# Block-sparse sample attention on one core: gathers, scores and denominators placed anew

## The chip, the cores and the metric

The kernel runs on one core of a Trainium2 chip. The metric is the device time of one execution in microseconds (us), less being better. The program is one inference step of a two-layer decoder trunk, for a prompt of 512 tokens and a sample group of 8 sequences with 8 new tokens each. All data are f32.

Names of the engines: PE (TensorE, matmuls and transposes through the identity), DVE (VectorE), ACT (ScalarE), POOL (GpSimd, which also issues the gathers), SP (SyncE, which issues the plain DMAs). Each engine runs its own instructions strictly in order; semaphores tie them together.

## The reference, cut to what matters

The change touches the sample half of branch B: compressed keys, selected blocks of 64 rows, and a window of 512 rows, each a softmax attention of its own.

```python
def ab_sample(...):
    kcf = concatenate([gather_pages(cc_k, page_table), kc])      # 4096 past rows of each sequence
    o_cmp, p_cmp = cmp_attend(qb, compress(kcf, pe_k, w1_k, w2_k), compress(vcf, ...), qpos)
    idx = select_blocks(p_cmp, qpos, ...)                        # the 16 best blocks for each query
    o_slc = slc_sample(qb, cs_k, cs_v, ks, vs, page_table, idx, qpos, sl_b)
    o_win = win_sample(qb, kwb, vwb, qpos, past_len, sl_b)

def compress(k, pe, w1, w2):      # blocks of 32 rows, flattened
    return silu((k + pe) @ w1) @ w2

def masked_softmax(s, valid):
    m = max(s); p = where(valid, exp(s - m), 0); den = sum(p)
    return p / den, m, den
```

## The kernel before

The stages follow one another, with a barrier between them: projection, prompt attention, sample attention A, then `compress_sample` (L1163), `attend_sample_b` (L1313), then the merge of the branches, the recurrence of layer 1 and the output projection. The change lies in the two named ones.

**compress_sample.** There are 16 units: 8 sequences, keys and values. For each, POOL gathers 4096 rows (2 MB, one indirect DMA with the page indices `idx`, L1202) into one of two buffers and regroups them by KV head (L1188); PE transposes them (L1230) and multiplies them with the compression weights (L1239). POOL issues a gather two units ahead; at the last two units it issues none.

**attend_sample_b.** The keys of the selected blocks are not gathered one by one: for every sequence b all 4096 rows of K and V are fetched (`xk`, `xv`, 2 MB each, two buffers each, L1417), and rows outside the 16 chosen blocks get a bias of -1e30. The work is a software pipeline of passes. In pass b, PE

- turns the keys of sequence b: eight groups of 512 rows (`keys`, L1468) and the window (`window_keys`, L1475), PSUM banks `bT`, copied to SBUF by DVE (groups 0, 1, 2, 3, 5, 7) or ACT (4, 6 and the window);
- computes their scores (`scores`, 128x512 in three banks `bS`, L1491, "w" for the window L1488, "n" for the new tokens L1485);
- turns the softmax weights of sequence b-1 (`turn`, L1498) out of `sc`, and multiplies them with its values (`weigh`, L1522; `weigh_rest` for window, new tokens and compressed blocks, L1532 to L1542);
- prepares the choice of blocks of sequence b+1 (`blocks` L1455, `groups` L1459).

DVE adds the bias to every score group and takes its minimum (`add_bias`, L1726, into `sc`), forms `nmax` (L1774, L1775), and for sequence b+1 the probabilities (`block_weights`, L1700, L1701) and the choice (`select`, L1706 to L1717). ACT takes the exponentials (`exp`, L1623, two groups each) and copies banks. POOL builds the bias `bd` of sequence b+1 (eight instructions, L1429) and issues the gathers. `outputs` (L1740 to L1745) divides by the denominators `den`, `den4`, of which there is one set.

The order is written out by hand in each engine's program, and the list `fills` gives the order in which `bT` banks are used. In pass b the scores of groups 0 to 3 stand on PE between the last weights' turns, "w", "n" and 4 to 7 stand at its end. `sc` holds one sequence: DVE may write the scores of b only when the weights of b-1 have been turned out of it, for which it waits once, for the last turn ("Pn").

At the stage's start SP loads the queries, old keys (`setup_in`) and five tables (`const_ready`), then the windows; POOL issues four gathers (K and V of sequences 0 and 1) at once. PE waits for `setup_in`, turns the queries, and then needs `const_ready`.

## Time and profile before

| what | us |
|---|---|
| median of 3 runs (2525.16 to 2527.83) | 2526.34 |
| the profiled execution, its own time | 2522.46 |
| its span | 2520.7 |
| PE busy in the span | 2228.4 |
| compress_sample (PE's first to last matmul) | 1057.5 to 1238.0 |
| attend_sample_b (PE's first to last matmul) | 1264.8 to 1499.1 |

PE is busy for 88% of the span, DVE 34%, ACT 28%, POOL 13%. Below, a "pass" begins where `blocks` (L1455) of the next sequence begins on PE. Columns of a timeline row: start in us, length in us, engine, line, operation, output<-inputs, shape, count; in brackets the idle time of that engine just before it and who ended it. A line of n instructions merged is followed by xn.

### The profile page before, as it was taken

To read this page: it belongs to the slowest core of one execution; us is meant where nothing else is said; L and a number is where in the kernel's file an instruction comes from. 1 tells how busy PE (TensorE), PEld (TensorE's weight loads), DVE (VectorE), ACT (ScalarE), POOL (GpSimd) and SP (SyncE) were. 2 spreads that over 40 slices of the span, in tenths; PEclk is the share of its full clock that TensorE was granted. 3 is DMA by queue.
4 is the path that set the end of the run, shared out by engine and by line. 5 is a ranking of instruction groups with operands and counts; after the bars stand their busy time and mean duration, and the time that the engine had idled before them with its cause. 6 is when DMAs were issued, how large, how long until landed. Compare 5 with 4: busy or idle time off the path is not lost. (4 is left out here: it accounts for less than half of the span.)

```text
span 2520.7 us, 34463 instructions
## 1 busy us (share of the span) xinstructions
PE 2228.4 (88%) x13652; PEld 1359.5 (54%) x13652; DVE 854.5 (34%) x2146; ACT 717.1 (28%) x1452; POOL 315.9 (13%) x393
## 2 busy tenths in 40 slices
PE   6999999478897788599679979969999999999798
PEld 3444454364444566488556654436666666566443
DVE  0000000025664344233254422324545444454322
ACT  0001000025664323122135430013444434343300
POOL 0000001103453000144143311000000000000000
PEclk9999999659999899799889989979999999999899
DMA  3232322302112999655334429048988897989710
GB/s 110 75 107 103 80 73 64 58 19 66 51 39 79 415 406 411 243 210 201 119 142 167 156 76 250 0 93 254 290 260 291 248 297 251 300 257 323 251 74 21
DMA packets 207823, 436.87 MB, mean 173 GB/s; under 512 B 59744, under 2 KB 162992, under 8 KB 191024
## 3 DMA queue, kind: packets, MB, share of 16 engines
q1 hardware_dynamic: 199856, 359.29, 43.8%
q0 software_dynamic: 7808, 75.39, 7.9%
q8 instruction: 109, 1.79, 0.3%
q14 instruction: 50, 0.41, 0.1%
HBM read 410.04 MB, written 163.13 MB: 227 GB/s over the span
## 5 line engine op out<-in xcount | busy, mean ns | idle before, releaser
L1901 PE MATMUL rec_bR<-x1T,rec_w 128*128 128x512 f32 x768 | 355.6, 618 | 0.0
L1901 PEld LDWEIGHTS rec_bR<-x1T,rec_w 128*128 128x128 f32 x768 | 147.4, 197 | 172.1 <-issue 171.1
L230 PE MATMUL pab_acc<-xT,pab_w 128*128 128x512 f32 x512 | 224.1, 598 | 10.0 <-DMA pab_w<-in_w_in_ab 10.0
L230 PEld LDWEIGHTS pab_acc<-xT,pab_w 128*128 128x128 f32 x512 | 97.4, 192 | 132.9 <-issue 122.7
L1136 DVE MEMSET kc_p<- 128x32 f32 x1 | 0.1, 85 | 471.2 <-PE cmpp_bP L1082 471.2
L234 PE MATMUL pab_acc<-pab_w,xT 128*128 128x512 f32 (+1 forms) x384 | 155.3, 565 | 0.0
L1239 PE MATMUL cmp_bH<-cmp_xT,cmp_w 128*128 128x256 f32 x512 | 131.5, 382 | 0.0
L548 ACT ACTIVATE ap_sc<-ap_sc,ap_nmax 128x128 f32<-128x128 f32 (+1 forms) x192 | 106.2, 554 | 84.3 <-DVE ap_nmax L578 83.1
L726 PE MATMUL mab_acc<-mab_w,mab_hT 128*128 128x512 f32 x256 | 114.8, 608 | 12.7 <-DMA mab_hT<-scratch_h 12.7
L2276 PE MATMUL out_acc<-out_w,oT 128*128 128x512 f32 x256 | 112.3, 601 | 13.5 <-DMA out_w<-in_w_out_c 13.5
L887 PE MATMUL sa_bT<-ident,sa_ring 128*128 128x128 f32 x640 | 88.8, 298 | 33.2 <-DMA sa_ring<-in_cache_a_k 24.2
L1910 PE MATMUL rec_bR<-rec_w,x1T 128*128 128x128 f32 x1024 | 117.0, 275 | 0.0
L1910 PEld LDWEIGHTS rec_bR<-rec_w,x1T 128*128 128x128 f32 x1024 | 115.7, 192 | 0.5 <-issue 0.5
L234 PEld LDWEIGHTS pab_acc<-pab_w,xT 128*128 128x128 f32 x384 | 72.5, 190 | 80.5 <-issue 80.5
L2105 POOL TENSOR_TENSOR rec_v_own<-rec_rows,rec_row_own 64x512 f32<-64x512 f32 x16 | 16.5, 1032 | 779.4 <-PE rec_bX L1960 631.7
L578 DVE CUSTOM_DVE_ANT_0 ap_sc<-ap_bS,ap_bias 128x128 f32<-128x128 f32 (+1 forms) x192 | 86.5, 488 | 68.4 <-PE ap_bS L493 32.9
L887 PEld LDWEIGHTS sa_bT<-ident,sa_ring 128*128 128x128 f32 x640 | 79.0, 154 | 44.3 <-DMA sa_ring<-in_cache_a_k 27.7
L516 PE MATMUL ap_bT<-ident,ap_sc 128*128 128x128 f32 x480 | 73.7, 285 | 30.2 <-ACT ap_pT L563 18.7
L1230 PE MATMUL cmp_bT<-ident,cmp_xg 128*128 128x128 f32 x512 | 78.8, 281 | 22.6 <-POOL cmp_xg L1188 20.6
L516 PEld LDWEIGHTS ap_bT<-ident,ap_sc 128*128 128x128 f32 x480 | 53.0, 143 | 75.9 <-POOL ap_sc L612 69.4
L1274 DVE COPY cmp_xT<-cmp_bT 128x512 f32<-128x512 f32 x80 | 55.3, 692 | 112.2 <-PE cmp_bT L1230 112.2
L1239 PEld LDWEIGHTS cmp_bH<-cmp_xT,cmp_w 128*128 128x128 f32 x512 | 88.7, 192 | 7.1
(368 smaller groups left out, 3448.2 us busy)
## 6 DMA issues: line engine op xcount, KB each, us to landing
out<-in_cache_a_k SPq DMA_DIRECT2D x8, 8160.0 KB, 29.7
out<-in_cache_a_v SPq DMA_DIRECT2D x8, 8160.0 KB, 29.6
sa_ring<-in_cache_a_k SPq DMA_DIRECT2D x40, 1024.0 KB, 12.6
sa_ring<-in_cache_a_v SPq DMA_DIRECT2D x40, 1024.0 KB, 20.4
rec_w<-in_w_in_c SPq DMA_DIRECT2D x64, 512.0 KB, 6.8
pab_w<-in_w_in_ab SPq DMA_DIRECT2D x8, 2048.0 KB, 8.1
pab_w<-in_w_in_ab SPq DMA_DIRECT2D x64, 128.0 KB, 3.3
ap_bias<-in_bias_p SPq DMA_DIRECT2D x16, 512.0 KB, 4.2
```

The costliest lines, as they stand in the source:

```text
L230: last = nc.tensor.matmul(acc[a % 8][:, :], w[u][:, k, j * P:(j + 1) * P], xT[:, k, 0:SEQ], start=(k == 0), stop=(k == KD - 1))
L234: last = nc.tensor.matmul(acc[a % 8][:, 0:width], xT[:, k, j * P:(j + 1) * P], w[u][:, k, 0:width], start=(k == 0), stop=(k == KD - 1))
L516: last = nc.tensor.transpose(bT[h][:, j * P:(j + 1) * P], sc[(i - LAG) % RING][h][:, j * P:(j + 1) * P], ident[:, :])
L548: nc.scalar.activation(at, at, ACT.Exp, bias=nmax[:, i % RING, h:h + 1], scale=-1.0, accum_out=den[:, i % RING, h:h + 1]).then_inc(exp_don ...
L578: nc.vector.tensor_tensor_reduce(out=sc[i % RING][h][:, 0:cols], in0=bS[i % 2][h][:, 0:cols], in1=bias[grp % 2][:, h, SEQ - cols:SEQ], sca ...
L726: last = nc.tensor.matmul(acc[m % 2][half][:, :], hT[:, k, m * P:(m + 1) * P], w[:, k, 512 * half:512 * half + 512], start=(k == 0), stop= ...
L887: last = nc.tensor.transpose(bank[:, (2 * jj + t) * P:(2 * jj + t + 1) * P], ring[at % RING][:, t, j * P:(j + 1) * P], ident[:, :])
L1230: last = nc.tensor.transpose(bT[f % 4][:, j * P:(j + 1) * P], xg[u][:, g, k * P:(k + 1) * P], ident[:, :])
L1239: last = nc.tensor.matmul(bH[i % 2][:, 0:KVB * P], w1[i % 2][:, k, :], xT[i % 2][:, k, :, :].rearrange("p g n -> p (g n)"), start=(k == 0) ...
L1901: last = nc.tensor.matmul(bank[:, :], w[h % 2][:, at, k, :], xT[:, k, 0:SEQ], start=(k == 0), stop=(k == KD - 1))
L1910: last = nc.tensor.matmul(bank[:, m * P:(m + 1) * P], xT[:, k, m * P:(m + 1) * P], w[h % 2][:, V_AT, k, :], start=(k == 0), stop=(k == KD ...
L2276: last = nc.tensor.matmul(acc[m % 2][half][:, :], oT[:, k, m * P:(m + 1) * P], w[:, k, 512 * half:512 * half + 512], start=(k == 0), stop= ...
```

## The change

1. **Gathers of sequence 0.** Where `compress_sample` issued no gather (its last two units), POOL now gathers K and V of sequence 0 of the selected branch into two tensors `first_k`, `first_v`, which live over both stages and serve as buffer 0 of `xk`, `xv`. In `attend_sample_b` POOL waits for `const_ready` and `setup_in` and then issues the two gathers of sequence 1.
2. **Order of the scores.** PE's loop over the eight groups is now: turn the weights of b-1, turn the keys of b, scores of the group before, weigh the group before. The scores run 0 to 7, then "w", "n"; `weigh(b-1, 7)` and `weigh_rest` stand at the pass's end.
3. **Finer waits.** `add_bias(b, j)` waits for the turn of group j of sequence b-1, not for the last turn. On DVE the adds stand between the copies of keys, `outputs(b-1)` stands behind `nmax` of b.
4. **Two sets of denominators** (`den4`, `den`): `exp` waits for the outputs of two sequences back.

```diff
@@ compress_sample, gpsimd
                     if i + 2 < NU:
                         pool.wait_ge(grouped[u], 2 * b + 2)
                         gather(i + 2)
+                    else:
+                        pool.indirect_dma_start(first[u][:, :, :].rearrange("p c k -> p (c k)"), None,
+                                                next_rows[u].rearrange("e n (s c) g d -> (e n s) (c g d)", c=CB),
+                                                bass.IndirectOffsetOnAxis(ap=idx[:, 0:1], axis=0)).then_inc(first_in[u], 16)
@@ attend_sample_b
-        xk, xv = ([s.sb(f"{n}{u}", [P, NKT, P]) for u in range(2)] for n in ("xk", "xv"))
+        xk, xv = ([x, s.sb(n, [P, NKT, P])] for x, n in zip(first, ("xk1", "xv1")))
-        den4, den, rden, cden = s.sb("den4", [P, 4]), s.sb("den", [P, 3]), s.sb("rden", [P, 3]), s.sb("cden", [P, 2])
+        den4, den, rden, cden = s.sb("den4", [P, 2, 4]), s.sb("den", [P, 2, 3]), s.sb("rden", [P, 3]), s.sb("cden", [P, 2])
-        SCORES = (0, 1, 2, 3, "w", "n", 4, 5, 6, 7)
+        SCORES = (0, 1, 2, 3, 4, 5, 6, 7, "w", "n")
@@ gpsimd
-                for b in range(2):
-                    gather(b, xk, pool_rows[0], xk_in)
-                    gather(b, xv, pool_rows[1], xv_in)
                 pool.wait_ge(const_ready, 16 * 5)
+                pool.wait_ge(setup_in, 16 * 4)
+                for x, rows, ready in ((xk, pool_rows[0], xk_in), (xv, pool_rows[1], xv_in)):
+                    gather(1, x, rows, ready)
@@ tensor, after keys(b, 0..2)
+                    for j in range(TC):
                         if before:
                             turn(b - 1, j)
+                        if mine and j < 5:
                             keys(b, 3 + j)
+                        if mine and j == 5:
+                            window_keys(b)
+                        if mine and j >= 1:
+                            scores(b, j - 1)
                         if before and j >= 1:
                             weigh(b - 1, j - 1)
+                        if after and j == 2:
+                            groups(b + 1)
                     if before:
                         turn_window(b - 1)
+                        turn_new(b - 1)
                     if mine:
+                        for j in (7, "w", "n"):
+                            scores(b, j)
                     if before:
                         weigh(b - 1, 7)
                         weigh_rest(b - 1)
@@ scalar
-                        if b >= 2:
-                            act.wait_ge(o_read, b - 1)
+                        if b >= 3:
+                            act.wait_ge(o_read, b - 2)
@@ vector, add_bias
+                    if b >= 1:
+                        dve.wait_ge(turned, number[{"w": ("Pw", b - 1, 0), "n": ("Pn", b - 1, 0)}.get(j, ("P", b - 1, j))] + 1)
@@ vector, a pass
                         copy_keys(b, 3)
+                        add_bias(b, 0)
                         copy_keys(b, 5)
+                        add_bias(b, 1)
                     if after:
                         select(b + 1)
                     if mine:
+                        add_bias(b, 2)
                         copy_keys(b, 7)
-                        if b >= 1:
-                            dve.wait_ge(turned, number["Pn", b - 1, 0] + 1)
-                        for j in SCORES[:4]:
-                            add_bias(b, j)
-                    if before:
-                        outputs(b - 1)
-                    if mine:
-                        for j in SCORES[4:]:
+                        for j in SCORES[3:]:
                             add_bias(b, j)
                         dve.wait_ge(s_read, len(SCORES) * (b + 1))
                         line(nc.vector.tensor_reduce(nmax[:, 1:2], low_w[:, :], AX_X, ALU.min))
                         nc.vector.tensor_reduce(nmax[:, 0:1], low[:, :], AX_X, ALU.min).then_inc(max_ready, 1)
+                    if before:
+                        outputs(b - 1)
```

How POOL's program stands at the seam of the two stages, before (`cmp_xg` is the regrouped input of the compression, `sb_xk0` buffer 0 of the keys):

```order
L1188 COPY cmp_xg1<-cmp_x1 128x2048 x2
L1190 UNCONDITIONAL_BRANCH
L1414 UNCONDITIONAL_BRANCH
L1417 DMA sb_xk0<-in_cache_b_slc_k,page_idx 128x4096
L1417 DMA sb_xv0<-in_cache_b_slc_v,page_idx 128x4096
L1417 DMA sb_xk1<-in_cache_b_slc_k,page_idx 128x4096
L1417 DMA sb_xv1<-in_cache_b_slc_v,page_idx 128x4096
L1429 TENSOR_TENSOR sb_bd0<-sb_ad,sb_slope_c 128x512 x8
```

and now:

```order
L1189 COPY cmp_xg0<-cmp_x0 128x2048 x2
L1219 DMA first_k<-in_cache_b_slc_k,page_idx 128x4096
L1189 COPY cmp_xg1<-cmp_x1 128x2048 x2
L1219 DMA first_v<-in_cache_b_slc_v,page_idx 128x4096
L1191 UNCONDITIONAL_BRANCH
L1420 UNCONDITIONAL_BRANCH
L1423 DMA sb_xk1<-in_cache_b_slc_k,page_idx 128x4096
L1423 DMA sb_xv1<-in_cache_b_slc_v,page_idx 128x4096
L1435 TENSOR_TENSOR sb_bd0<-sb_ad,sb_slope_c 128x512 x8
```

Two of the four gathers have moved into the stage before.

PE at the end of a middle pass before, from the last weighing of groups to the blocks of the next pass (`sb_pT` are turned weights, `sb_bS` banks of scores):

```order
L1522 MATMUL sb_bO<-sb_xv1,sb_pT3 64x64 x8
L1510 MATMUL sb_bT1<-ident,sb_sc 8x128
L1511 MATMUL sb_bT1<-ident,sb_sc_w 8x128
L1491 MATMUL sb_bS0<-sb_kT,sb_qd 128x512
L1532 MATMUL sb_bO<-sb_v_new1,sb_pT_n 64x64 x2
L1536 MATMUL sb_bO<-sb_xwv1,sb_pT_w 64x64 x8
L1539 MATMUL sb_bO<-sb_v_new1,sb_pT_n 64x64 x2
L1542 MATMUL sb_bO<-vc,sb_pT_c2 64x64 x2
L1488 MATMUL sb_bS1<-sb_kT_w,sb_qd 128x512
L1485 MATMUL sb_bS2<-sb_kT_new,sb_qd 128x8 x2
L1491 MATMUL sb_bS0<-sb_kT,sb_qd 128x512
L1491 MATMUL sb_bS1<-sb_kT,sb_qd 128x512
```

and now:

```order
L1497 MATMUL sb_bS0<-sb_kT,sb_qd 128x512
L1528 MATMUL sb_bO<-sb_xv1,sb_pT2 64x64 x8
L1511 MATMUL sb_bT0<-ident,sb_sc_w 128x128 x4
L1516 MATMUL sb_bT1<-ident,sb_sc 8x128
L1517 MATMUL sb_bT1<-ident,sb_sc_w 8x128
L1497 MATMUL sb_bS1<-sb_kT,sb_qd 128x512
L1494 MATMUL sb_bS2<-sb_kT_w,sb_qd 128x512
L1491 MATMUL sb_bS0<-sb_kT_new,sb_qd 128x8 x2
L1528 MATMUL sb_bO<-sb_xv1,sb_pT3 64x64 x8
L1538 MATMUL sb_bO<-sb_v_new1,sb_pT_n 64x64 x2
L1542 MATMUL sb_bO<-sb_xwv1,sb_pT_w 64x64 x8
L1545 MATMUL sb_bO<-sb_v_new1,sb_pT_n 64x64 x2
```

The last scores now stand ahead of the last weighings, and only three score groups are left there.

DVE around the end of a middle pass, before:

```order
L1726 ISA sb_sc,sb_low<-sb_bS,sb_bd 128x512
L1726 ISA sb_low 128x1
L1774 TENSOR_REDUCE sb_nmax<-sb_low_w 128x1
L1775 TENSOR_REDUCE sb_nmax<-sb_low 128x1
L1695 TENSOR_REDUCE sb_cmax<-sb_bM 128x1
L1691 COPY sb_kT<-sb_bT 128x512 x3
L1699 RECIPROCAL sb_cden<-sb_cden 128x1
L1700 TENSOR_SCALAR sb_pc<-sb_pc,sb_cden 128x128
L1701 SCALAR_TENSOR_TENSOR sb_pc<-sb_pc 128x128
L1691 COPY sb_kT<-sb_bT 128x512 x2
```

and now:

```order
L1758 TENSOR_REDUCE sb_nmax<-sb_low_w 128x1
L1759 TENSOR_REDUCE sb_nmax<-sb_low 128x1
L1728 TENSOR_REDUCE sb_den<-sb_den 128x1
L1729 RECIPROCAL sb_rden<-sb_den 128x3
L1733 TENSOR_TENSOR sb_ob<-sb_bO,sb_rden 128x192
L1680 TENSOR_REDUCE sb_cmax<-sb_bM 128x1
L1676 COPY sb_kT<-sb_bT 128x512 x3
L1684 RECIPROCAL sb_cden<-sb_cden 128x1
L1685 TENSOR_SCALAR sb_pc<-sb_pc,sb_cden 128x128
L1686 SCALAR_TENSOR_TENSOR sb_pc<-sb_pc 128x128
L1676 COPY sb_kT<-sb_bT 128x512
L1711 ISA sb_sc,sb_low<-sb_bS,sb_bd 128x512
```

The outputs have moved to between `nmax` and `cmax`, and the first add of a pass stands behind the fourth copy of keys.

## Rows read from the trace of the kernel before

**Rows 1.** Windows: us; busy PE, PEld, DVE, ACT, POOL; PE clock; DMA share; GB/s.
```profile
1170.00:1238.00 68.00, 67.41 (x407) 59.44 (x405) 21.21 (x38) 13.27 (x24) 16.82 (x10) 1.00 0.23 90
...
1240.00:1270.00 30.00, 2.12 (x12) 1.64 (x12) 2.94 (x9) 1.17 (x3) 3.77 (x4) 0.50 0.90 341
...
1367.00:1394.00 27.00, 24.68 (x243) 16.64 (x239) 12.97 (x49) 12.78 (x26) 9.12 (x10) 1.00 0.47 175
```

**Rows 2.** Timeline of the start of attend_sample_b and its pass 0.
```profile
1240.78 1.27 SPq L1386 DMA_DIRECT2D sb_k_old<-scratch_z  x2
...
1244.46 0.48 SPq L1388 DMA_DIRECT2D sb_group<-in_group_sum  x1
...
1264.76 1.11 PE L1547 MATMUL sb_bS<-ident,sb_q 64*128 64x64 f32 x8 [26.79 <-DMA sb_k_old<-scratch_z]
...
1268.05 0.79 PE L1455 MATMUL sb_bM<-kc,sb_qd 128*128 128x128 f32 x2 [1.96 <-DVEq L1678]
...
1271.82 0.79 PE L1455 MATMUL sb_bM<-kc,sb_qd 128*128 128x128 f32 x2 [0.17 <-DVE sb_score L1706]
...
1289.13 0.38 PE L1455 MATMUL sb_bM<-kc,sb_qd 128*128 128x128 f32 x2
```

**Rows 3.** Issue to landing, by tile: sb_q (two DMAs), sb_k_old (two), sb_xk (eight).
```profile
DMA to landing us min/median/max: 2.9/8.3/13.7
...
DMA to landing us min/median/max: 18.0/20.6/23.3
...
DMA to landing us min/median/max: 8.0/8.6/17.1
```

**Rows 4.** DMA views: an earlier stage's load, KB each and us to landing; SP's queue 1238:1270.
```profile
sa_k_new<-scratch_z SPq DMA_DIRECT2D x1, 256.0 KB, 4.1
...
q1 hardware_dynamic: 2576, 1.81, 18.9%
```

**Rows 5.** PE's timeline around the middle pass 1372.47 to 1400.25.
```profile
1366.23 0.33 PE L1532 MATMUL sb_bO<-sb_v_new,sb_pT_n 8*64 8x64 f32 x4
...
1367.63 1.12 PE L1488 MATMUL sb_bS<-sb_kT_w,sb_qd 128*128 128x512 f32 x2
...
1368.95 3.68 PE L1491 MATMUL sb_bS<-sb_kT,sb_qd 128*128 128x512 f32 x8
1372.47 0.39 PE L1455 MATMUL sb_bM<-kc,sb_qd 128*128 128x128 f32 x2
...
1375.63 0.66 PE L1498 MATMUL sb_bT<-ident,sb_sc 128*128 128x128 f32 x4 [1.46 <-ACT sb_sc L1623]
...
1385.59 0.66 PE L1498 MATMUL sb_bT<-ident,sb_sc 128*128 128x128 f32 x4
...
1387.65 0.65 PE L1498 MATMUL sb_bT<-ident,sb_sc 128*128 128x128 f32 x4
...
1392.95 1.12 PE L1491 MATMUL sb_bS<-sb_kT,sb_qd 128*128 128x512 f32 x2 [0.79 <-DVE sb_low L1726]
...
1400.25 0.39 PE L1455 MATMUL sb_bM<-kc,sb_qd 128*128 128x128 f32 x2
```

**Rows 6.** Timelines of DVE, ACT and POOL in the same pass.
```profile
1373.67 0.28 DVE L1695 TENSOR_REDUCE sb_cmax<-sb_bM 128x1 f32<-128x128 f32 x1
...
1376.17 0.29 DVE L1701 SCALAR_TENSOR_TENSOR sb_pc<-sb_pc 128x128 f32<-128x128 f32 x1
...
1374.34 1.14 ACT L1623 ACTIVATE sb_sc<-sb_sc,sb_nmax 128x1024 f32<-128x1024 f32 x1
...
1393.09 2.04 POOL L1429 TENSOR_TENSOR sb_bd<-sb_ad,sb_slope_c 128x512 f32<-128x512 f32 x2
```

**Rows 7.** Timeline of pass 0, where POOL builds bd beside DVE.
```profile
1273.70 8.06 POOL L1429 TENSOR_TENSOR sb_bd<-sb_ad,sb_slope_c 128x512 f32<-128x512 f32 x8 [28.94 <-DVE sb_ad L1717]
...
1276.85 1.03 DVE L1701 SCALAR_TENSOR_TENSOR sb_pc<-sb_pc 128x128 f32<-128x128 f32 x1
```

**Rows 8.** Timeline of the last pass, which has no keys and scores.
```profile
1485.07 1.68 PE L1498 MATMUL sb_bT<-ident,sb_sc 128*128 128x128 f32 x8 [2.45 <-ACT sb_sc L1623]
```

More of the change, by code:

```diff
@@ L1160, in _, with compress_sample @@
                     last.then_inc(m_read, 1)
-def compress_sample(nc, pools, idx, weights, pe_bias, kc, vc, ident):
+def compress_sample(nc, pools, idx, weights, pe_bias, kc, vc, next_rows, first, first_in, ident):
     NCHUNK, NU, FILLS = CB * HD // P, 2 * NB, 8
@@ L1310, in _, with attend_sample_b @@
                             result(i - 2)
-def attend_sample_b(nc, z, pools, idx, win_k, win_v, kc, vc, o_cmp, o_slc, o_win, ident, consts):
+def attend_sample_b(nc, z, pools, idx, win_k, win_v, first, first_in, kc, vc, o_cmp, o_slc, o_win, ident, consts):
     NKT, TC, GONE = CB, 8, -2e4
@@ L1347, in attend_sample_b @@
         w_in, stored, copied = ([s.sem(f"{n}{u}") for u in range(2)] for n in ("w_in", "stored", "copied"))
[L1348 removed]
+        xk_in, xv_in = ([sem, s.pool_dma_sem(n)] for sem, n in zip(first_in, ("xk1_in", "xv1_in")))
         setup, turned, scored, s_read, weighed, o_done, o_read = (
@@ L1622, in exp @@
                     c = slice(1024 * i, 1024 * i + 1024 + (NT if i == 3 else 0))
-                    nc.scalar.activation(sc[:, c], sc[:, c], ACT.Exp, bias=nmax[:, 0:1], scale=-1.0, accum_out=den4[:, i:i + 1]).then_inc(exp_done, 1)
+                    nc.scalar.activation(sc[:, c], sc[:, c], ACT.Exp, bias=nmax[:, 0:1], scale=-1.0, accum_out=den4[:, b % 2, i:i + 1]).then_inc(exp_done, 1)
                 for b in range(-1, NB + 1):
@@ L1650, in _ @@
                     if before:
-                        nc.scalar.activation(sc_w[:, :], sc_w[:, :], ACT.Exp, bias=nmax[:, 1:2], scale=-1.0, accum_out=den[:, 2:3]).then_inc(exp_done, 1)
+                        nc.scalar.activation(sc_w[:, :], sc_w[:, :], ACT.Exp, bias=nmax[:, 1:2], scale=-1.0, accum_out=den[:, (b - 1) % 2, 2:3]).then_inc(exp_done, 1)
                         copy_weights(b - 1, 4)
@@ L2387, in build @@
             vc = s.enter_context(nc.sbuf_tensor("vc", [P, NB, P], F32))
-            compress_sample(nc, (d["cache_b_cmp_k"], d["cache_b_cmp_v"]), idx, cmp_weights, pe_bias, kc, vc, ident)
-            attend_sample_b(nc, d["z"], (d["cache_b_slc_k"], d["cache_b_slc_v"]), idx, d["cache_b_win_k"], d["cache_b_win_v"],
+            next_rows = (d["cache_b_slc_k"], d["cache_b_slc_v"])
+            first = [s.enter_context(nc.sbuf_tensor(f"first_{n}", [P, CB, P], F32)) for n in "kv"]
+            first_in = [top.enter_context(nc.semaphore(f"first_{n}_in")) for n in "kv"]
+            compress_sample(nc, (d["cache_b_cmp_k"], d["cache_b_cmp_v"]), idx, cmp_weights, pe_bias, kc, vc, next_rows, first, first_in, ident)
+            attend_sample_b(nc, d["z"], next_rows, idx, d["cache_b_win_k"], d["cache_b_win_v"], first, first_in,
                             kc, vc, d["ocmp"], d["oslc"], d["owin"], ident, d)
```

39 lines of the change are left out of this document (3 added, 36 removed).

## The prediction, made before the changed kernel was run

> **What bounds the kernel now.** The share of busy time comes first: over the span PE is busy for 88%, so a gain must come from places where PE stands. The windows show three regimes around the change [rows 1]. In compress_sample PE is busy for 67.4 of 68 us, POOL for 16.8, and the DMA share is 0.23: PE bounds it, and POOL and the DMA engines have room. Between the stages, 1240 to 1270, PE is busy for 2.1 of 30 us while the DMA share is 0.90: here the transfers decide. In a middle pass PE is busy for 24.7 of 27 us at the full granted clock (1.00); the next engines are DVE with 13.0 and ACT with 12.8. So PE's program is the bound there, and only its pauses can go.
>
> The pauses at the start: PE waits 26.79 us for the second load of k_old, from 1238.0 to 1264.76 [rows 2]. It was issued at about 1241.4 and landed 23.3 us later, the first load of q, ahead of the gathers, in 2.9 us [rows 3]. What lies between is 8 MB of gathers. From PE's first setup matmul to the start of pass 0 it is 7.1 us, of which 3.3 to the first `blocks`; pass 0 takes 1289.13 - 1271.82 = 17.3 us.
>
> The pauses of a middle pass, T = 1372.47 to 1400.25, 27.78 us [rows 5]: 1.46 us before the first turn of weights, for the exponential, and 0.79 us before the fourth score, since DVE gets the first three only when the last weights are turned. Both come back in each pass 1 to 6 at the same length. In the last pass PE waits 2.45 us for the exponential [rows 8].
>
> **The change part by part.**
>
> *Gathers of sequence 0 in the compression: cost nothing.* Two more indirect DMAs for POOL, at most 1.2 us each to issue (between a weighing's end and `bd` stand one gather and its waits, [rows 6]), where its work fills a quarter of the time, and 4 MB for DMA engines that are three quarters idle [rows 1]. They stand behind the regrouping of the last two units; a unit of the 16 takes some 11 us and a regrouping runs about two units ahead of its matmuls, so both land, in 8.0 to 17.1 us [rows 3], before the stage ends. PE's work covers them; without that cover they would cost 2.4 us.
>
> *The start of attend_sample_b.* SP's small loads now meet no gather, since POOL issues those of sequence 1 only when all have landed. A landing with little beside it took 2.9 us [rows 3] or 4.1 us [rows 4]. I take the longer: k_old lands at 1241.4 + 4.1 = 1245.5 and the first `blocks` comes 3.3 us later, at 1248.8. The tables have to be there by then as well: the last is issued at 1244.46 [rows 2], plus 4.1 gives 1248.6, so the two meet. `blocks` stood at 1268.05: gain 19.3 us. Bounds: with 2.9 us for both, 1247.6, gain 20.5. From the other side: all of SP's packets of this stretch took 18.9% of 16 engines over 32 us [rows 4], 6.0 us if nothing else runs; the tables then land at 1250.5 at worst, gain 17.5. The granted clock of PE is 0.50 from 1240 on [rows 1], 2 us after its last matmul, so it will have fallen in a pause of 7 us too: no gain from it in pass 0.
>
> What becomes late next: the gathers of sequence 1, issued at about 1249, land by 1249 + 17.1 = 1266 at worst [rows 3]; their keys are needed at the start of pass 1, 1252.6 + 15.9 = 1268.5. The window of sequence 0 (0.5 MB, SP) is beside them; PE wants it some 9.6 us into pass 0, at 1262. At 341 GB/s [rows 1], 4.2 + 1.0 MB are through 15 us after 1249; if the windows came last, PE would wait 2 us. They are queued earlier, so I take 0 and keep 2 for the range.
>
> *Pass 0.* Its limit is POOL's bias: eight instructions end 8.06 us after 1273.70 [rows 7], T0 + 9.9, and `select` of sequence 1, which waits for all of them, stands on DVE before every add. Two of the eight adds now stand in front of it. From T0 + 10.2 six adds, the seventh copy, window and new tokens remain on DVE, about 5.5 us, and PE ends one score behind: 15.9 us for 17.3, gain 1.4, between 0 (if PE has the same work left) and 2.5.
>
> *Middle passes, PE.* The instructions are the same, in another order. Step prices: turn, score, weigh take 1387.65 - 1385.59 = 2.06 us; `weigh_rest` 1.40; window and new scores 1.32 [rows 5]. The wait of 0.79 us goes: a score now comes at most once in 2.1 to 2.6 us, an add takes 0.7, and three banks lie between; with it goes the restart of the pipeline, some 0.2. The wait of 1.46 us shrinks but stays. ACT's exponential stands behind that of sequence b+1's probabilities, which waits for cmax, which waits for `blocks`. Before, cmax began at T + 1.20 and the exponential at T + 1.87 [rows 6], because `nmax` was in front of cmax. Now `nmax` is done at about T - 0.9: behind the last group score PE still has 1.32 (w, n) + 0.62 (weigh) + 1.40 (rest) = 3.3 us, and DVE needs 2.4. But `outputs`, which waits for the last matmul of the pass, now precedes cmax: it ends at about T + 0.53, and cmax can start at T + 0.55. That is 0.65 earlier; the wait becomes 0.8. Sum: 0.79 + 0.2 + 0.65 = 1.6, and small waits for banks copied by ACT in the dense first third, which the scores now loosen, 0.2 (bounds 0 and 0.5). Gain 1.8 us in each of six passes, 10.8; bounds 1.2 and 2.5, so 7 to 15.
>
> *The new waits.* An add waits for the turn of its own group of b-1. PE turns group j one step ahead of score j-1, so this wait ends before the score does: nothing. Behind a waiting add stand a copy of keys and `select`. K3's copy is the tight one: the turn of weights 2 needs its bank at about T + 6.1.
>
> *POOL's bias moves against DVE.* The order behind `weigh(b-1, 7)` (gather of values, then `bd`) is as before: 1.2 us after that weighing ends, `bd` begins [rows 6]. The weighing now ends at T - 1.4 and not 7 us before T, so `bd` runs from T - 0.2 to T + 7.9, over `block_weights` (T + 3.2). In this pass, with POOL idle, L1701 took 0.29 us; in pass 0 beside `bd` it took 1.03 [rows 6, 7]. With as much again for L1700, K3's copy ends at T + 6.0 and not T + 4.9: just in time. I take 0. The Trainium skill ("SBUF — State Buffer", section "SBUF: two separate sides") says that VectorE with two SBUF inputs or in a two-port mode and GpSimd share a port pair under an exclusive lock, and the loser stands for the whole instruction. The two rows agree. By that rule each of the two DVE steps can stand behind one whole `bd` instruction, and the sum would be that of rival 1.
>
> *Pass 7 and 8.* Pass 7 prepares no sequence, so no cmax stands before its exponential: of its waits some 2.1 us go. In pass 8 `nmax` is ready before PE has ended pass 7; of the 2.45 us, 0.4 stay: gain 2.0, bounds 1.5 and 2.4. The second set of denominators takes away a wait of ACT that was never last; it only allows `outputs` to stand where it does: 0.
>
> *Sum.* 19.3 + 1.4 + 10.8 + 2.1 + 2.0 = 35.6 us. Span 2520.7 - 35.6 = 2485.1; the profiled execution 2522.46 would be 2486.9. The median lies 3.9 us above that execution: 2526.3 - 35.6 = **2490.7 us**. What follows (merge, recurrence) starts behind a barrier and only shifts.
>
> **The rivals.**
>
> 1. *POOL's lock eats at the passes.* Each `bd` is 8.06 / 8 = 1.0 us. If both DVE steps stand for a whole one, K3's copy ends at T + 6.9 and PE waits 0.7 to 0.8 in six passes: +4 to 5 us, 2495. For it: L1701 at 1.03 [rows 7]. Against: copies out of PSUM kept their time in pass 0. Chance 0.12.
> 2. *The passes gain nothing*: a new wait, for the exponential or a bank, takes the place of those removed. Only the start and pass 0 remain, 20.7 us: 2505.6. For it: the same ring of `nmax`, exponential and turn closes each pass. Against: 3.3 us of PE work now lie between. Chance 0.10.
> 3. *The start is not shortened*: the small rows of q and the tables are slow by themselves, the gathers not their cause. Then 16.3 us remain: 2510. Against: 2.9 against 23.3 us in the same queue [rows 3]. Chance 0.08.
> 4. *Slower, by lockstep.* DVE's adds now stand between copies that PE needs. If DVE falls three scores behind (its add ends more than 7 us after the score), every step carries the hop to DVE, the add and the hop back, about 1.2 us; 8 steps in 7 passes are 67 us, the 14.9 of the passes are lost, and the time is 2573. It decides only if DVE's 13 us a pass, plus 8.06 of `bd` in full, were over 25 us; they are 21. Chance 0.05.
> 5. *More is gained*: PE runs without any wait in the passes, some 25 us each: another 5 to 7 us, 2484. Chance 0.10.
>
> **How the numbers follow.** The forecast has 0.55, its own range is 2485 to 2497 (17.5 to 20.5, less up to 2; 0 to 2.5; 7 to 15; 3 to 5). The range 2482 to 2507 takes in rivals 1, 2 and 5 and leaves out 3 and 4 and the tails. A measurement of this kernel tells some 0.2% (5 us) from no change. Faster by more 0.93, within 0.02, slower 0.05.
>
> **What would show it right or wrong.** PE's first setup matmul at 1245 to 1246, `blocks` at about 1249, and a DMA share near nothing for long in 1250 to 1270 but for 4 MB; k_old's landing at 3 to 4 us. Passes of about 26.0 us, with 0.8 us before the first turn of weights and no wait for `sb_low`; L1701 near 1 us in all passes; pass 8's first turn without 2.45. Compression unchanged at 180.5 us. Wrong would be: a wait on `sb_xwk` or `sb_xk` in the first two passes, waits on `sb_kT` copies in each, or k_old still landing after 10 us.

## The result, and the profile after

| | median, us (range) | ratio to before, 95% interval |
|---|---|---|
| before | 2527.09 (2525.16 to 2527.85) | |
| changed | 2500.95 (2497.82 to 2502.86) | 0.9897 [0.9879, 0.9914] |

The changed kernel is 26 us faster. The forecast was a time of 2490.7 us: the measured one lies in the range (2482 to 2507), with 10 us less gained than forecast. The profiled execution of the changed kernel took 2502.86 us, its span 2501.1.

**The start went as forecast, and a little further.** Timeline of the start of attend_sample_b after the change (start, length, engine, line, operation; idle time before it in brackets):

```profile
1240.70 1.26 SPq L1392 DMA_DIRECT2D sb_k_old<-scratch_z  x2
...
1243.60 1.11 PE L1553 MATMUL sb_bS<-ident,sb_q 64*128 64x64 f32 x8 [5.70 <-DMA sb_k_old<-scratch_z]
...
1246.88 0.79 PE L1461 MATMUL sb_bM<-kc,sb_qd 128*128 128x128 f32 x2 [1.96 <-DVEq L1663]
...
1246.87 0.94 POOL L1423 DMA_INDIRECT sb_xk<-in_cache_b_slc_k,page_idx  x1 [35.10 <-DMA sb_group<-in_group_sum]
```

DMA issues of the changed kernel between 1235 and 1265 (KB each, median us from issue to landing):

```profile
sb_k_old<-scratch_z SPq DMA_DIRECT2D x2, 32.0 KB, 2.4
...
sb_group<-in_group_sum SPq DMA_DIRECT2D x1, 64.0 KB, 2.5
...
sb_xk<-in_cache_b_slc_k,page_idx POOLq DMA_INDIRECT x1, 11.0
sb_xv<-in_cache_b_slc_v,page_idx POOLq DMA_INDIRECT x1, 14.6
```

With no gather beside them the loads of k_old land in 2.2 to 2.5 us where they took 18.0 to 23.3 [rows 3], and PE's wait falls from 26.79 us [rows 2] to 5.70. `blocks` stands at 1246.88 instead of 1268.05. POOL really issues the gathers of sequence 1 only then, and nobody waits for them.

**The passes did not.** Windows of the changed kernel: a stretch of the compression, pass 1, pass 2, pass 3, and a piece of pass 2 (us; busy PE, PEld, DVE, ACT, POOL; PE clock; DMA share; GB/s):

```profile
1200.00:1237.00 37.00, 36.67 (x215) 32.14 (x213) 10.45 (x19) 6.99 (x13) 5.64 (x4) 1.00 0.30 114
...
1266.00:1292.00 26.00, 24.73 (x259) 17.12 (x259) 14.46 (x57) 12.75 (x26) 5.17 (x7) 1.00 0.23 83
1292.00:1322.00 30.00, 26.31 (x259) 17.93 (x257) 18.52 (x50) 12.75 (x26) 9.84 (x11) 0.94 0.45 162
1322.00:1350.50 28.50, 24.80 (x261) 17.15 (x257) 18.56 (x50) 12.75 (x26) 9.91 (x11) 1.00 0.47 170
...
1303.00:1304.00 1.00, 1.00 (x7) 0.32 (x8) 0.21 (x1) 0.00 (x0) 0.00 (x0) 0.50 1.05 442
```

Pass 1 takes the 26.0 us that the prediction gave to all of them. Passes 2 to 6 take 30.06, 28.52, 30.11, 30.07 and 28.52. DVE is busy for 4 us more than in pass 1, and PE waits longer. In three of these five passes PE's own busy time is also 1.5 us longer, at a granted clock that falls to 0.50, the 1.2 GHz level, behind its pause. PE's waits between 1266 and 1439 in the changed kernel (us in total, times, longest):

```profile
PE sb_bT L1504 <- issue: 13.8, 5, 2.8
PE sb_bT L1504 <- ACT sb_sc L1608: 5.5, 6, 1.2
```

The second row is the wait that was forecast to stay (0.8 us a pass; it is 0.9, and 1.2 in pass 1). The first row is new: five times 2.8 us. Its place is the turn of weights 2 ("turn 2") in passes 2 to 6. PE, DVE and POOL around it in pass 2:

```profile
1297.71 0.69 PE L1528 MATMUL sb_bO<-sb_xv,sb_pT 128*64 128x64 f32 x16
1301.12 0.63 PE L1504 MATMUL sb_bT<-ident,sb_sc 128*128 128x128 f32 x4 [2.73 <-issue]
...
1294.93 5.05 DVE L1685 TENSOR_SCALAR sb_pc<-sb_pc,sb_cden 128x128 f32<-128x128 f32 x1
1300.02 0.36 DVE L1686 SCALAR_TENSOR_TENSOR sb_pc<-sb_pc 128x128 f32<-128x128 f32 x1
1300.30 0.68 DVE L1676 COPY sb_kT<-sb_bT 128x512 f32<-128x512 f32 x1
...
1291.88 8.01 POOL L1435 TENSOR_TENSOR sb_bd<-sb_ad,sb_slope_c 128x512 f32<-128x512 f32 x8
```

A DVE step that takes 0.29 us alone (L1685, the scaling of the block probabilities) takes 5.05 us here. It ends within 0.1 us of the end of POOL's run of eight bias instructions (1291.88 + 8.01 = 1299.89). The copy of keys 3 ("K3's copy", L1676) follows it on DVE, and turn 2 needs the bank that this copy reads. The profile ends the wait with "issue", but 1301.12 is 0.14 us behind the end of K3's copy, and a second trace of the same kernel (e_after, below) names that copy for it:

```profile
1302.41 1.09 PE L1504 MATMUL sb_bT<-ident,sb_sc 128*128 128x128 f32 x4 [2.93 <-DVE sb_kT L1676]
```

Pass 0 looks different, although POOL's run is there too:

```profile
1252.46 8.07 POOL L1435 TENSOR_TENSOR sb_bd<-sb_ad,sb_slope_c 128x512 f32<-128x512 f32 x8 [3.41 <-DVE sb_ad L1702]
...
1254.84 0.74 DVE L1685 TENSOR_SCALAR sb_pc<-sb_pc,sb_cden 128x128 f32<-128x128 f32 x1
1255.62 1.03 DVE L1686 SCALAR_TENSOR_TENSOR sb_pc<-sb_pc 128x128 f32<-128x128 f32 x1
```

Here each of the two steps lost no more than one POOL instruction of 1.0 us. That was the picture of [rows 7], and the prediction took it for all passes. Why the two differ was the question of the experiments.

### The profile page after: what moved, and what is told of

The parts are those of the page before. It is cut to its first block and busy times, and to the rows that moved or that the text cites. A ratio compares the mean times of both kernels' runs of the same rounds, so it can differ in the third digit from the quotient of the medians.

```text
span 2501.1 us, 34476 instructions
## 1 busy us (share of the span) xinstructions
PE 2231.9 (89%) x13652; PEld 1361.3 (54%) x13652; DVE 878.5 (35%) x2146; ACT 717.3 (29%) x1452; POOL 316.9 (13%) x393
## 5 line engine op out<-in xcount | busy, mean ns | idle before, releaser
L887 PEld LDWEIGHTS sa_bT<-ident,sa_ring 128*128 128x128 f32 x640 | 80.7, 156 | 43.2 <-DMA sa_ring<-in_cache_a_k 26.6
L963 DVE COPY sa_kT<-sa_bT 128x512 f32<-128x512 f32 x80 | 55.3, 692 | 103.9 <-PE sa_bT L887 91.7
```

The source lines that it names most:

```text
L887: last = nc.tensor.transpose(bank[:, (2 * jj + t) * P:(2 * jj + t + 1) * P], ring[at % RING][:, t, j * P:(j + 1) * P], ident[:, :])
```

## Experiments

**The changed kernel again, with three ways to keep the loss away.** e_after is the changed kernel. e_k3_first:

```diff
-                        for j in range(3):
+                        for j in range(4):
                             copy_keys(b, j)
                     if after:
                         block_weights(b + 1)
                     if mine:
-                        copy_keys(b, 3)
                         add_bias(b, 0)
```

e_bd_late, on POOL ahead of the run, then e_bd_gaps, behind each instruction of the run (L1434):

```diff
                     if b >= 2:
                         pool.wait_ge(s_read, score_no(b - 2, 7) + 1)
+                        if b + 1 < NB:
+                            pool.wait_ge(pc_ready, b + 2)
```

```diff
                                                 slope_c[:, 4 * j:4 * j + 4].unsqueeze(2).broadcast_to([P, 4, P]), ALU.add).then_inc(bd_ready, 1)
+                        pool.wait_ge(bd_ready, TC * b + j + 1)
```

> The changed kernel again, as the base of the other three on the same chip. The theory (DVE's scaling of pc, L1685, stands 5.05 us for POOL's run of bd in passes 2 to 6, and turn 2 of PE stands behind it through the copy of keys 3) expects the same picture: L1685 at 5.05 us, a pause of 2.75 us before turn 2 in five passes, time 2498 to 2503.

> The changed kernel with one edit on DVE: the copy of keys 3 stands ahead of block_weights. L1685 still stands 5 us for POOL. Theory (the pause on PE is the missing copy of keys 3): the pauses of 2.75 us and the falls of PE's clock behind them go, passes 2 to 6 take 26 to 26.5 us, 2481 to 2486 in all, 15 to 20 us less than the changed kernel. Rival (PE waits for something else that POOL's run delays, the probabilities for groups or a free score bank): the pause stays or moves to groups, and less than 5 us are gained.

> The changed kernel with one wait more: for sequences 2 to 6 POOL begins bd only when block_weights of the next sequence is done. Theory (POOL's run holds DVE's scaling): L1685 takes 0.29 us in every pass, the pauses go, the first add waits up to 0.5 us for its bias, 26.0 to 26.3 us a pass, 2481 to 2486. Rival (L1685 is long for another reason, such as the gather of values in flight, which is issued just before bd and lands as L1685 ends): the gather is still issued at the pass's end, so L1685 stays at 5 us and the time near 2500.

> The changed kernel with POOL waiting for its own increment after each of the eight bd instructions, so that they no longer follow back to back. Theory A (the port goes to POOL for as long as its instructions follow each other without a gap): L1685 falls from 5.05 to at most 1.3 us and the pauses go. Theory B (the port is decided instruction by instruction and the 5 us have another cause): L1685 stays at 5 us. bd itself gets longer by the waits, 8.0 to perhaps 9 us.

| | us | ratio to before | passes 2 to 4, us |
|---|---|---|---|
| e_after | 2502.63 (2498.67 to 2503.62) | 0.9908 [0.9894, 0.9921] | 30.1 |
| e_k3_first | 2483.61 (2481.55 to 2486.76) | 0.9837 [0.9823, 0.9851] | 25.75 |
| e_bd_late | 2483.86 (2479.37 to 2486.38) | 0.9834 [0.9819, 0.9849] | 25.53 |
| e_bd_gaps | 2478.48 (one run) | | 25.54 |

DVE in the pass at 1294 of e_k3_first, then of e_bd_late:

```profile
1297.99 3.61 DVE L1685 TENSOR_SCALAR sb_pc<-sb_pc,sb_cden 128x128 f32<-128x128 f32 x1
```

```profile
1297.30 0.29 DVE L1687 TENSOR_SCALAR sb_pc<-sb_pc,sb_cden 128x128 f32<-128x128 f32 x1
```

e_bd_gaps, the same place, DVE and POOL:

```profile
1291.69 0.33 DVE L1686 TENSOR_SCALAR sb_pc<-sb_pc,sb_cden 128x128 f32<-128x128 f32 x1
1292.06 1.15 DVE L1687 SCALAR_TENSOR_TENSOR sb_pc<-sb_pc 128x128 f32<-128x128 f32 x1
...
1288.66 8.88 POOL L1435 TENSOR_TENSOR sb_bd<-sb_ad,sb_slope_c 128x512 f32<-128x512 f32 x8
```

e_k3_first leaves DVE's long stand (it still ends with POOL's run) and only takes K3's copy out from behind it: the whole loss is gone, so the path bias run, DVE's step, K3's copy, turn 2 is shown. The price of that path is 2502.63 - 2483.61 = 19 us, give or take 5: the pauses of 13.8 us and some 1.5 us of slower clock in three passes are about 18 of them. e_bd_late takes the meeting away and gains the same. It also settles a rival: the gather of values is still issued at the pass's end (1293.30) and under way when DVE's step begins, and the step takes 0.29 us, so a gather in flight is not enough to hold it. e_bd_gaps keeps the meeting, and makes POOL wait for each of its own instructions: the step takes 0.33 us. If POOL gave the way free after each instruction in the changed kernel, the step there would have been about as short.

**The start alone, in the old order of the passes.** e_start is the kernel before, with the gathers of sequence 0 in the compression and POOL's waits for the setup (cut to the two places that matter):

```diff
+                    else:
+                        pool.indirect_dma_start(first[u][:, :, :].rearrange("p c k -> p (c k)"), None,
...
-                for b in range(2):
-                    gather(b, xk, pool_rows[0], xk_in)
-                    gather(b, xv, pool_rows[1], xv_in)
                 pool.wait_ge(const_ready, 16 * 5)
+                pool.wait_ge(setup_in, 16 * 4)
+                for x, rows, ready in ((xk, pool_rows[0], xk_in), (xv, pool_rows[1], xv_in)):
+                    gather(1, x, rows, ready)
```

> The kernel before, with part 1 of the change alone: the gathers of sequence 0 are issued inside the compression, those of sequence 1 only when the setup's four loads have landed; PE's, ACT's and DVE's orders and the denominators stay those of before. Theory (the start's gain is the transfers' alone and stands by itself): the setup on PE begins some 21 us earlier than in the kernel before, as in the changed kernel (1243.6 against 1264.8), the middle passes keep 27.8 us, and the time is the kernel before minus 20 to 21.5, ratio 0.9915 to 0.9925. Rival (part of the start's gain depends on the new order of the passes, or sequence 1's gathers, now landing beside pass 0, are awaited there): minus 17 or less, ratio 0.9935 or more, with a wait for xk1 or xv1 in pass 1.

2507.54 us (2501.99 to 2511.39), ratio 0.9925 [0.9910, 0.9940]: 19 us faster, with an interval of 15 to 23. PE's setup in e_start:

```profile
1245.35 1.11 PE L1551 MATMUL sb_bS<-ident,sb_q 64*128 64x64 f32 x8 [5.74 <-DMA sb_k_old<-scratch_z]
```

The wait is 21.0 us shorter than in [rows 2], the middle passes keep 27.78 us, and there is no wait for xk1 or xv1. The start's gain stands by itself. What the rest of the change brought as it was written is small: 2501 to 2503 against 2507.5, some 5 us, but the intervals of the ratios overlap, and by the traces it is under 2 us in this stage (22.6 us gained in the changed kernel, 21.0 of them at the start here).

**Is it the form of DVE's step, or its moment?** e_form writes the step with two inputs (`one` is a tile of ones), e_phase asks 0.4 us later within POOL's run (`pad` is a spare tile). The two ideas behind them are theory F, that only the one-input form is held, and rival P, that only the moment decides:

```diff
-                    line(nc.vector.tensor_scalar(pc[:, :], pc[:, :], cden[:, 1:2], None, ALU.mult))
+                    line(nc.vector.scalar_tensor_tensor(out=pc[:, :], in0=pc[:, :], scalar=cden[:, 1:2], in1=one[:, :],
+                                                        op0=ALU.mult, op1=ALU.mult))
```

```diff
                     dve.wait_ge(c_exp, b + 1)
+                    if b >= 1:
+                        for i in range(2):
+                            nc.vector.tensor_reduce(pad[:, i:i + 1], bM[:, 0:P], AX_X, ALU.max)
```

> The changed kernel, with the tensor_scalar on DVE that took 5.05 us in passes 2 to 6 written as a scalar_tensor_tensor with the same result (times a tile of ones; 128x128, two inputs from SBUF). Theory F (what stands for the whole run is the one-input form; the two-input form takes the port anew between POOL's instructions, as the next line did with 1.03 us in pass 0 and 1.15 in the run with gaps): the line takes 0.3 to 1.3 us, the next one about 1.0, turn 2 waits under 0.3 us, passes 2 to 6 take 25.5 to 26.2 us, and the time is 16 to 21 us under the changed kernel. Rival G (any DVE instruction on two SBUF operands stands until POOL's run ends, and pass 0 was a matter of its moment): the line takes about 5 us again, and the time is that of the changed kernel within 2 us.

> The changed kernel, with two extra maxima of the block scores (PSUM to a spare column, 0.2 to 0.3 us each) on DVE ahead of the reciprocal, in all passes but the first, so that the tensor_scalar starts 0.45 to 0.55 us later within POOL's run of bias instructions: in the middle of one of its 1.0-us instructions instead of 0.05 us behind the edge of one. Theory A (the port stays with POOL for a run without gaps, wherever DVE asks): the tensor_scalar still ends with the run, about 4.5 us instead of 5.05, passes 2 to 6 keep 28.5 to 30.1 us, the time is that of the changed kernel within 2 us. Rival P (the moment decides: asked for in the middle of an instruction, as in pass 0 where it took 0.74 us, the port is given at that instruction's end): 0.5 to 1.1 us, PE's pause gone, the time 14 to 19 us under the changed kernel.

The step in e_form, then in e_phase:

```profile
1300.22 5.12 DVE L1687 SCALAR_TENSOR_TENSOR sb_pc<-sb_pc,sb_cden,sb_one 128x128 f32<-128x128 f32 x1
```

```profile
1295.57 4.67 DVE L1689 TENSOR_SCALAR sb_pc<-sb_pc,sb_cden 128x128 f32<-128x128 f32 x1
```

2503.82 us (ratio 0.9909 [0.9895, 0.9924]) and 2503.83 (0.9907 [0.9893, 0.9922]): the changed kernel's time in both. Neither the form nor the moment decides; theory F and rival P fall. The step stands to the end of the run: DVE began it 3.05 us after the run's start (1294.93 against 1291.88) and in e_phase 3.4 us after it, and the step is shorter by that 0.4.

**The same meeting in the old order.** e_old_beside is the kernel before, with its bias run held by a wait until the next pass:

```diff
                         pool.wait_ge(s_read, score_no(b - 2, 7) + 1)
+                        if b + 1 < NB:
+                            pool.wait_ge(cmax_ready, b + 2)
```

> The kernel before, where POOL's eight bias instructions of a sequence wait in addition for the column maximum of the next sequence's block scores (cmax_ready), so that in passes 2 to 6 they start about 1.5 us into the next pass and run beside DVE's block weights, which in the kernel before ran with POOL idle (L1700 0.28 us, L1701 0.29). PE's, ACT's and DVE's orders are those of before. Theory (POOL keeps the shared port for as long as its instructions follow back to back, whatever the order of the passes): L1700 takes 4 to 7 us instead of 0.28 in these passes, ends with the run of bias instructions, PE stands for 2 to 4 us in each, and the time is 8 to 20 us over the kernel before. Rival (the long stand comes from the changed order or from how the run starts there, right behind a gather's issue): L1700 stays under 1.1 us, as in pass 0 of the changed kernel, and the time is within 3 us of the kernel before.

2526.61 us (2519.18 to 2535.21), ratio 1.0001 [0.9987, 1.0014]. POOL and DVE in its pass at 1374:

```profile
1375.95 8.06 POOL L1431 TENSOR_TENSOR sb_bd<-sb_ad,sb_slope_c 128x512 f32<-128x512 f32 x8 [8.84 <-DVE sb_cmax L1697]
...
1377.67 0.39 DVE L1702 TENSOR_SCALAR sb_pc<-sb_pc,sb_cden 128x128 f32<-128x128 f32 x1
1378.10 1.03 DVE L1703 SCALAR_TENSOR_TENSOR sb_pc<-sb_pc 128x128 f32<-128x128 f32 x1
```

My theory fell: eight instructions back to back, and DVE got its turn within the run. In pass 0, here and in e_one_gap below, the first step ends some 0.1 us behind the end of the POOL instruction that it met (worked out from the run's start and 1.0 us for each instruction). "POOL keeps the port as long as its instructions follow back to back" is not enough. What the quick cases have in common (pass 0, [rows 7], this one) is that the run began when a wait ended. In passes 2 to 6 of the changed kernel it began straight behind the issue of the gather of values: 1290.92 + 0.95 = 1291.87, and the run at 1291.88. That gave theory S, that a run which starts straight behind a gather's issue holds DVE's step to its end and one which starts behind a wait does not, and two kernels, one for each direction.

**How the run starts.** e_one_gap is the changed kernel with one short stop between the gather's issue and the run (POOL writes one element, `mark`, and waits for its own semaphore); e_old_behind is the kernel before with the gather held until the next pass, so that the run follows it directly:

```diff
                         pool.wait_ge(s_read, score_no(b - 2, 7) + 1)
+                        nc.gpsimd.memset(mark[:, 0:1], 0.0).then_inc(marked, 1)
+                        pool.wait_ge(marked, b - 1)
```

```diff
                         pool.wait_ge(weighed, TC * b)
+                        if b + 2 < NB:
+                            pool.wait_ge(cmax_ready, b + 3)
                         gather(b + 1, xv, pool_rows[1], xv_in)
```

> The changed kernel, where from sequence 2 on POOL, between the issue of a gather and its run of eight bias instructions, writes one element and waits for its own semaphore, so that the run starts behind a wait and not straight behind the gather; the eight instructions still follow back to back. Theory S (what decides is how the run starts: in pass 0, and in the old order with the run held for cmax, it began behind a wait and DVE got the port within 0.4 to 0.8 us; in passes 2 to 6 it began straight behind the gather's issue and DVE stood to its end): the tensor_scalar (L1687 here) takes 0.3 to 1.1 us, PE's pause at turn 2 is gone, passes 2 to 6 take 25.5 to 26.0 us, span some 18 us under the changed kernel (2480 to 2486). Rival T (it has to do with the moment of the pass or its neighbours, not with the start of the run): 4.5 to 5.1 us, passes of 28.5 to 30.1 us, span within 3 us of 2501.

> The kernel before, where POOL holds the gather of the next sequence's values until the next pass's cmax_ready, and its run of eight bias instructions then starts straight behind that gather's issue, beside DVE's block weights (the run held for cmax by a wait of its own gave L1702 0.39 us and L1703 1.03 us, and no loss of time). Theory S (a run that starts straight behind a gather keeps the port to its end, in the old order too): the tensor_scalar (L1700 here) takes 6 to 7.5 us in these passes instead of 0.28, PE stands 2 to 4 us in each, and the span is 10 to 20 us over the kernel before. Rival T (the new order of the passes is needed for it): under 1.1 us, span within 3 us of the kernel before.

POOL and DVE in the pass at 1316 of e_one_gap:

```profile
1315.57 0.94 POOL L1424 DMA_INDIRECT sb_xv<-in_cache_b_slc_v,page_idx  x1 [15.40 <-PE sb_bO L1531]
1316.51 0.11 POOL L1435 MEMSET sb_mark<- 128x1 f32 x1
1316.70 8.09 POOL L1438 TENSOR_TENSOR sb_bd<-sb_ad,sb_slope_c 128x512 f32<-128x512 f32 x8
...
1319.56 0.29 DVE L1688 TENSOR_SCALAR sb_pc<-sb_pc,sb_cden 128x128 f32<-128x128 f32 x1
1319.89 1.01 DVE L1689 SCALAR_TENSOR_TENSOR sb_pc<-sb_pc 128x128 f32<-128x128 f32 x1
```

POOL, DVE and PE in the pass at 1352.5 of e_old_behind, and a window of PE's clock behind the pause:

```profile
1354.79 0.94 POOL L1417 DMA_INDIRECT sb_xv<-in_cache_b_slc_v,page_idx  x1 [25.89 <-DVE sb_cmax L1697]
1355.74 8.01 POOL L1429 TENSOR_TENSOR sb_bd<-sb_ad,sb_slope_c 128x512 f32<-128x512 f32 x8
...
1356.08 7.76 DVE L1702 TENSOR_SCALAR sb_pc<-sb_pc,sb_cden 128x128 f32<-128x128 f32 x1
...
1364.98 1.08 PE L1500 MATMUL sb_bT<-ident,sb_sc 128*128 128x128 f32 x4 [6.41 <-DVE sb_kT L1693]
...
1366.00:1370.00 4.00, 4.00 (x31) 3.55 (x30) 1.79 (x12) 1.64 (x3) 0.00 (x0) 0.50 0.83 352
```

One execution each: e_one_gap 2481.36 us, span 2479.6, with passes of 25.7; e_old_behind 2564.84, span 2563.0, with passes 2 to 6 of 36 to 37 us instead of 27.78. That is 42 us over the span of the kernel before (2520.7), and 37 over the median of its runs beside this one (2528.22). Both directions bear theory S out, in each of the five passes. The size expected for e_old_behind was wrong (10 to 20 us): a pause of 6.4 us per pass, and the clock at 0.50 for more than 4 us behind it, make over 8 us a pass. One short stop of POOL costs 0.2 us a pass, and passes 2 to 6 of e_one_gap together take 18.7 us less than in the changed kernel.

In e_one_gap, in e_bd_late and in the changed kernel DVE's step begins 3.05 to 3.06 us behind the end of the gather's issue. The age of the gather is thus the same in the quick and in the long case, and what differs is POOL: idle, stopped once, or not stopped. e_bd_gaps fits this too, since its run also starts straight behind the issue but stops after its first instruction. Whether the wait or the small write in e_one_gap made the difference was not tried apart.

**Versions that go on from there.** e_bd_early turns POOL's order, so that the bias of a sequence comes ahead of the gather of its values; e_best also puts ACT's first exponential ahead of that of the block scores:

```diff
+                    if b >= 2:
+                        pool.wait_ge(weighed, TC * (b - 1))
+                        gather(b, xv, pool_rows[1], xv_in)
                     if b >= 1 and b + 1 < NB:
                         pool.wait_ge(turned, number["K", b - 1, 7] + 1)
                         gather(b + 1, xk, pool_rows[0], xk_in)
-                        pool.wait_ge(weighed, TC * b)
-                        gather(b + 1, xv, pool_rows[1], xv_in)
```

```diff
-                    if after:
-                        act.wait_ge(cmax_ready, b + 2)
-                        nc.scalar.activation(pc[:, :], bM[:, 0:P], ACT.Exp, bias=cmax[:, :], accum_out=cden[:, 0:1]).then_inc(c_exp, 1)
                     if before:
                         act.wait_ge(max_ready, b)
...
                         exp(b - 1, 0)
+                    if after:
+                        act.wait_ge(cmax_ready, b + 2)
+                        nc.scalar.activation(pc[:, :], bM[:, 0:P], ACT.Exp, bias=cmax[:, :], accum_out=cden[:, 0:1]).then_inc(c_exp, 1)
+                    if before:
                         exp(b - 1, 1)
```

> The changed kernel, with POOL's order turned: from sequence 2 on the bias of a sequence is made ahead of the gather of its values instead of behind it, so that it runs in the middle of the pass before, right after the select (about 11 to 20 us into the pass), and not beside DVE's block weights. Theory (the loss was the meeting of the two alone): the tensor_scalar takes 0.29 us in every pass but the first, passes 2 to 6 take 25.4 to 25.8 us as in the run with the bias held for pc_ready (25.53), and the time is 16 to 21 us under the changed kernel, ratio to before 0.982 to 0.985. Rival (beside the middle of the pass the run takes the port from DVE's biased scores or from the select's steps): DVE instructions of L1711 or L1694 to L1702 of over 1 us, passes of 26.0 us or more.

> e_bd_early, with ScalarE's first exponentials of a pass (those of the sequence before, which wait for max_ready) ahead of the exponentials of the block scores, which wait for DVE's cmax behind the outputs. Theory (PE's wait of 0.7 to 0.85 us ahead of turn 0 is ACT's order: cmax, block exponentials, then exp 0): the wait goes, passes 1 to 6 take 24.7 to 25.1 us, the time is 4 to 5 us under e_bd_early, ratio to before 0.9805 to 0.983. Rival (the block exponentials now come later and block_weights, ahead of K3's copy on DVE, with them): a new wait of PE at turn 2 of 0.3 us or more, and no gain within 1 us.

e_bd_early: 2486.24 us (2481.17 to 2490.41), ratio 0.9845 [0.9826, 0.9864]. e_best: 2484.19 (2477.35 to 2487.57), 0.9825 [0.9805, 0.9845]. Both beat the kernel before and the changed one, and neither can be told from e_k3_first or e_bd_late. DVE's step takes 0.29 us in every pass but the first, as expected, but the passes take 26.4 and 25.9 us instead of 25.4 to 25.8 and 24.7 to 25.1. It is not what the rival of e_bd_early had in mind: DVE's scores beside the bias run keep their 0.69 us. DVE, POOL and PE at the start of a pass of e_bd_early:

```profile
1313.26 0.34 PE L1549 MATMUL sb_bO<-vc,sb_pT_c 128*64 128x64 f32 x4
...
1313.74 0.93 POOL L1423 DMA_INDIRECT first_k<-in_cache_b_slc_k,page_idx  x1 [0.30 <-issue]
...
1314.65 0.36 DVE L1734 TENSOR_TENSOR sb_ob<-sb_bO,sb_rden 128x192 f32<-128x192 f32 x1 [1.85 <-PE sb_bO L1549]
...
1316.88 0.66 PE L1505 MATMUL sb_bT<-ident,sb_sc 128*128 128x128 f32 x4 [1.56 <-ACT sb_sc L1609]
```

`outputs` multiplies 1.05 us after the matmul that it waits for, where 0.35 is usual, and begins where POOL's second gather issue ends (1313.74 + 0.93 = 1314.67); cmax and the exponential follow it. In e_best, PE's wait is then for K0 to K2's copies behind the same multiplication (1.07 us). That the two gather issues in a row hold it back is read from the traces and was not tried by itself. ACT's order with e_bd_late's POOL was not run either.

## Why the prediction was right or wrong, step by step

- **Gathers in the compression cost nothing: right.** PE is busy 36.67 of 37 us there, at a granted clock of 1.00, the same share as before [rows 1], and its last matmul of the stage ends at 1237.9 (1238.0 before).
- **Start, 19.3 us: right, 2 us too small.** 21.2 in the trace, 21.0 in e_start. Of the two landings at hand I took the longer, 4.1 us; 2.4 came. The lower bound for the time (2.9 us) was nearer. The bound of 17.5, with all of SP's packets in a row, did not bite. PE's granted clock stayed low there (0.61 over 1238 to 1250.7), as said.
- **Pass 0, 1.4: right**, 2.0 (15.3 us for 17.3).
- **Middle passes, 1.8 each: right for what was reckoned, and overturned by what was put at nothing.** The wait for `sb_low` is gone, the wait for the exponential is 0.9, and pass 1 takes 26.0 us as forecast. With the meeting taken away all take 25.5. The step that failed is "I take 0" for the bias run beside DVE's block weights. Rival 1 named the mechanism and the chain to K3's copy and turn 2, but gave DVE one POOL instruction for each of its steps, 0.7 to 0.8 us on PE. It is 2.8 us on PE in passes 2 to 6 and, in three of these five, 1.5 us of slower clock: passes 1 to 6 together lost 6.6 us against [rows 5]'s 27.78 each, where 10.8 were to be gained. The row it was priced by, pass 0 in [rows 7], was a run that started behind a wait; the runs in question would start straight behind a gather's issue. [rows 6] show that place, with POOL's run at 1393.09, but with DVE's block weights nowhere near it. The step also has a slip of its own: "as much again for L1700" is 2 x 0.74 = 1.5 us, which puts K3's copy at T + 6.4 and not T + 6.0, 0.3 us behind the T + 6.1 that turn 2 needs. The price of the mechanism as assumed was small but not 0.
- **The page that was cited.** The Trainium skill ("SBUF — State Buffer", section "SBUF: two separate sides") has the loser of the shared port pair stand for the whole instruction of the other. Pass 0, e_old_beside and e_one_gap agree (0.28 to 1.03 us against POOL's 1.0); passes 2 to 6 and e_old_behind do not (5.05 and 7.76 us, five and nearly eight of POOL's instructions). The measurement decides.
- **Pass 7, 2.1: right**, 2.3 (24.3 for 26.6). **Pass 8, 2.0: too small**, 3.7 (13.0 for 16.7). The wait fell from 2.45 us [rows 8] to 0.27. I had left out that PE's clock fell behind the old wait. The same stretch in the kernel before, as a window:

```profile
1485.00:1489.00 4.00, 3.92 (x32) 3.10 (x34) 0.00 (x0) 3.34 (x7) 0.00 (x0) 0.57 0.00 0
```

  0.57 of full speed there, 1.00 in the last pass of the changed kernel: 1.5 us.
- **Sum.** At the end of attend_sample_b the trace has 22.6 us where 35.6 were forecast: 21.2 + 2.0 - 6.6 + 2.3 + 3.7. In the profiled executions 3.0 us of them are lost again behind the stage, in work that the change doesn't touch; the changed kernel's executions differ by 5 us among themselves. The medians differ by 26.
- **That the time lies in the range is in part luck.** The term of the passes lies far out of its bounds (7 to 15 us forecast, 6.6 lost). The range went up to 2507 for rival 1, the same meeting at 4 to 5 us instead of the 18 to 19 that it cost, and for rival 2, which did not come; the other terms gave 4.4 us more than forecast, and the medians show 26 us where the profiled spans show 19.6. The narrower range of the forecast alone was given as 2485 to 2497, but the bounds listed for it add up to gains of 25.5 to 43 us, so 2483 to 2501; the measured time lies outside the one and at the edge of the other.
- **With the failed step made good.** e_k3_first and e_bd_late land 41 us under the kernel before: rival 5's size, since 5 to 6 us more than forecast came from the start, pass 8 and passes of 25.5 us.

## What to carry to other kernels

A cost taken at nothing needs a row in which the two instructions meet in the same way: the same instruction on the other engine, started from the same kind of predecessor, not just somewhere beside it. Where GpSimd does a run of elementwise work, look at what precedes it. If it is a gather's issue and VectorE works between two SBUF tiles meanwhile, give the run a wait of its own to start from, or take what PE needs out from behind the VectorE step. And a pause of PE is not paid once: behind 2.8 us it cost 1.5 more in three of five places, behind 6.4 us the passes were longer by 1.5 to 2.7 us more than the pause.
